# Input projections of a two-layer trunk: dense tiles or steps between the products of the heads

## What is computed

```python
def trunk_layer(x, cond, layer, lp, rope, ctx):
    mod = cond @ lp['w_mod'] + lp['b_mod']
    sh1, sc1, g1, sh2, sc2, g2 = jnp.split(mod[:, None, :], 6, axis=-1)
    hmix = rmsnorm(x, lp['norm1_g']) * (1 + sc1) + sh1
    mix, new_ctx = token_mixers(hmix, layer, lp, rope, ctx)
    x = x + g1 * mix
    hffn = rmsnorm(x, lp['norm2_g']) * (1 + sc2) + sh2
    gate, up = jnp.split(hffn @ lp['w_ffn_in'], 2, axis=-1)
    x = x + g2 * ((jax.nn.silu(gate) * up) @ lp['w_ffn_out'])
    return x, new_ctx

def token_mixers(h, layer, lp, rope, ctx):
    (q_a, k_a, v_a, beta_a, alpha_a, z_a, q_b, k_b, v_b, u_c, gate_logits) = split_columns(h @ lp['w_in'])
    ...
    o_a, s_fin = gated_deltanet(q_a, k_a, v_a, beta_a, alpha_a, z_a, ...)
    o_b, kv = differential_attention(q_b, k_b, v_b, ...)
    o_c = hyena(u_c, ...)
    g_a, g_b, g_c = jnp.split(jax.nn.sigmoid(gate_logits), 3, axis=-1)
    merged = g_a * (o_a @ lp['w_br_a']) + g_b * (o_b @ lp['w_br_b']) + g_c * (o_c @ lp['w_br_c'])
    out = merged @ lp['w_out']
```

## Time and profile before

| what | value |
|---|---|
| median of 3 runs | 4095.87 us (4094.25 to 4096.15) |
| span of the profiled execution | 4092.7 us (3.2 us below the median) |
| PE busy | 3457.7 us, 84% |
| PE's weight loads | 3089.2 us, 75% |
| DVE busy | 1412.5 us, 35% |
| POOL busy | 1435.3 us, 35% |
| ACT busy | 841.8 us, 21% |

### The profile page before, as it was taken

The page is one execution under the profiler, slowest core; times in us unless marked ns, Lnnn a source line. Parts: engine busy times, 40 slices in busy tenths (PEclk is TensorE's granted clock), DMA queues, the critical chain, the costliest instruction groups (busy, mean ns, idle before and its releaser), DMA issues.

```text
span 4092.7 us, 61740 instructions
## 1 busy us (share of the span) xinstructions
PE 3457.7 (84%) x21792; PEld 3089.2 (75%) x21792; DVE 1412.5 (35%) x2231; ACT 841.8 (21%) x1657; POOL 1435.3 (35%) x1088
## 2 busy tenths in 40 slices
PE   6978887777889987999987788887687899799997
PEld 5967767535659987999977676784374799799996
DVE  2066663255531222111122666614553412211112
ACT  3133332232111112000022333313312111210001
POOL 0444442002205543444424444320131255254443
PEclk8988898877799998999988999987787999899998
DMA  4201111111102211222211111111111122121221
GB/s 159 75 29 42 41 41 62 55 41 50 58 27 72 77 66 48 72 72 70 75 64 51 43 41 41 41 62 54 41 55 49 37 77 72 41 77 67 71 73 67
DMA packets 62782, 240.94 MB, mean 59 GB/s; under 512 B 6960, under 2 KB 6960, under 8 KB 61488
## 3 DMA queue, kind: packets, MB, share of 16 engines
q1 hardware_dynamic: 60336, 224.77, 15.9%
q10 hardware_dynamic: 1728, 12.36, 0.8%
q0 software_dynamic: 576, 2.10, 0.1%
HBM read 234.48 MB, written 4.72 MB: 58 GB/s over the span
## 4 chain that ended last, share of the span: by engine, by line
PE 69%; DVE 16%; issue 6%; DVEq 4%; ACT 2%; POOL 1%; ACTq 1%; POOLq 1%; DMA 0%; SPq 0%
PE ps_G L583 26%; PE ps_GPM L583 25%; DVE whi_room L1564 3%; PE ps_GPM L614 3%; DVE outs L1636 2%; PE ps_M L967 2%; DVE outs L1632 2%; PE ps_G L852 1%; DVE small L1756 1%; PE ps_M L909 1%; PE ps_M L891 1%; PE ps_M L664 1%; PE ps_M L995 1%; DVE big L1787 1%; DVEq L1453 1%
## 5 line engine op out<-in xcount | busy, mean ns | idle before, releaser
L1973 POOL CAST w_hi<-ring 128x1024 fp32r<-128x1024 f32 x296 | 309.0, 1044 | 1620.8 <-PE ps_G L583 1002.4
L1975 POOL TENSOR_TENSOR w_lo<-ring,w_hi 128x1024 fp32r<-128x1024 f32 x296 | 740.3, 2501 | 51.1 <-issue 9.1
L583 PE MATMUL ps_G<-room_a,w_hi 128*128 128x320 f32 x1984 | 457.9, 320 | 100.1 <-DVEq L1453 65.4
L583 PE MATMUL ps_GPM<-room_a,w_hi 128*128 128x320 f32 x1984 | 437.5, 309 | 0.0
L583 PEld LDWEIGHTS ps_G<-room_a,w_hi 128*128 128x128 f32 x1984 | 348.5, 197 | 103.0 <-issue 103.0
L583 PE MATMUL ps_G<-room_b,w_hi 128*128 128x320 f32 x1408 | 368.4, 314 | 26.4 <-DVEq L1453 26.4
L583 PE MATMUL ps_G<-room_o,w_hi 128*128 128x320 f32 x1280 | 337.2, 313 | 45.6 <-DVEq L1453 45.6
L583 PE MATMUL ps_GPM<-room_b,w_hi 128*128 128x320 f32 x1408 | 361.4, 309 | 0.0
L583 PE MATMUL ps_GPM<-room_o,w_hi 128*128 128x320 f32 x1280 | 332.9, 309 | 0.0
L583 PEld LDWEIGHTS ps_GPM<-room_a,w_hi 128*128 128x128 f32 x1984 | 331.8, 188 | 0.0
L2027 POOL TENSOR_TENSOR outs<-big,con 128x512 f32<-128x512 f32 x168 | 207.7, 1237 | 350.1 <-DVEq L1602 230.9
(11 more groups left out here) (393 smaller groups left out, 6006.8 us busy)
## 6 DMA issues: line engine op xcount, KB each, us to landing
ring<-in_W SPq DMA_DIRECT2D x416, 512.0 KB, 3.2
big<-in_INV ACTq DMA_DIRECT2D x2, 1664.0 KB, 6.6
par<-in_PARAMS ACTq DMA_DIRECT2D x2, 1646.0 KB, 7.8
big<-in_FWD ACTq DMA_DIRECT2D x2, 1632.0 KB, 8.3
x<-in_X SPq DMA_DIRECT2D x1, 2560.0 KB, 8.8
out_Y<-h SPq DMA_DIRECT2D x1, 2560.0 KB, 7.6
con<-in_CONSTS SPq DMA_DIRECT2D x1, 1364.0 KB, 11.6
sc<-in_HYCS ACTq DMA_DIRECT2D x2, 578.5 KB, 3.7
```

The source lines that it names most:

```text
L583: m = pe.matmul(ap, w[wi][:, k, n0:n0 + P], acts[ai][k][:, a:b], start=(k == 0 and i == 0), stop=(k == chunks - 1 and i == 2))
L1973: nc.gpsimd.tensor_copy(hi, raw)
L1975: nc.gpsimd.tensor_tensor(wlo[:, slot * UNIT:(slot + 1) * UNIT], raw, hi.bitcast(F32), ALU.subtract)
```

## The change

The units are dealt out anew, and with them the places of the products. h's parts get rooms for a whole layer (`h_hi`, `h_lo`), made once at each norm, tile by tile: DVE scales a tile, ACT shifts and rounds it, DVE takes the rest two tiles later; PE's first tile waits chunk by chunk. `round_tiles` and `low_tiles` are gone: A, B, C and mix read the same parts. Each branch's o gets rooms too, and `merged` gets its parts per pair of tiles during the last third of mix; out's first tile waits chunk by chunk. The first third of mix writes `merged` where it was added to zeros before.

Stage A has 7 dense tiles (q, k, v of head 0 and 1 and z of head 0). The other tiles of A, all of B and the values (four tiles by channel, transposed later per head) are 21 tiles that `projection_steps` divides into steps of three matmuls. Delta heads carry 64 steps each, attention heads 0 and 1 32 each and head 2 16. They use one pair of PSUM banks (`G0`, `G1`), which ACT empties by halves (`first_half`, `second_half`). Both sets of heads are written out instead of looped over. The last delta head makes no convolutions, norms and reciprocals; there DVE rotates for attention head 0, before the reciprocal of the output norm. Scores keep two pairs of banks.

Modulation units leave the delta heads (8 each) and stand in norm 1 (8), attention heads 0 to 3 (4, 4, 8, 8), norm 2 (4) and the last step of each f1 group (4 each, between its tiles). `f2`'s first tile waits for its activations chunk by chunk. GpSimd splits two units before a head's levels, one after level 3, one after the last level, then makes the next head's growth factors. The state is stored per head from ACT's queue (before, once by POOL), the rope table is loaded from ACT's queue in the last delta head. In the Hyena stage the eight products of its gate (`gv`) come before the filter's arguments on DVE, and two tables are loaded earlier.

```diff
-    return [("A", 4, "wwww"), ("delta", H, "m" * 8), ("B", 2, "wwww"), ("V", 1, "wwww"), ("attn", H, "mmmm"),
-            ("C", 3, "wwww"), ("mix", 3, "w" * 12), ("out", 2, "wwww"),
-            ("f1_0", 4, "wwww"), ("f2_0", 2, "wwww"), ("f1_1", 4, "wwww"), ("f2_1", 2, "wwww"),
-            ("f1_2", 3, "wwww"), ("f2_2", 2, "wwww")]
+    return [("n1", 1, "m" * 8), ("A0", 1, "w" * 7), ("D0", 1, "wwww"), ("D1", 1, "wwww"), ("D2", 1, "wwww"),
+            ("D3", 1, "wwww"), ("T0", 1, "wmmwmm"), ("T1", 1, "wmmwmm"), ("T2", 1, "w" + "m" * 8), ("T3", 1, "m" * 8),
+            ("C", 3, "wwww"), ("mix0", 1, "w" * 12), ("mix1", 1, "w" * 12), ("mix2", 1, "w" * 12), ("out", 2, "wwww"),
+            ("n2", 1, "mmmm"), ("f1_0", 3, "wwww"), ("fx_0", 1, "wwmmwwmm"), ("f2_0", 2, "wwww"),
+            ("f1_1", 3, "wwww"), ("fx_1", 1, "wwmmwwmm"), ("f2_1", 2, "wwww"),
+            ("f1_2", 2, "wwww"), ("fx_2", 1, "wwmmwwmm"), ("f2_2", 2, "wwww")]
...
-SCORE_BANKS = [("M0", "M1"), ("M2", "M3"), ("G0", "G1")]
-
-ROTATIONS = [("rot_q", "G0"), ("rot_k", "G1")]
+SCORE_BANKS = [("M0", "M1"), ("M2", "M3")]
...
+            def projection_steps(phase, units, fills, first_fill, layer):
+
+
+                def run(a, b):
+                    for s in range(a, b):
+                        u, half, k = s // 16, (s // 8) % 2, s % 8
+                        w = parts(phase, units[u], layer)
+                        if half == 0:
+                            to, lo_, hi_ = over_banks[0][:, 0:HALF], 0, HALF
+                        else:
+                            to, lo_, hi_ = over_banks[0][:, HALF:NT], HALF, NT
+                        if k == 0:
+                            _, fl = fill(fills, "ab"[half], layer, first_fill + u)
+                        for i, (wi, ai) in enumerate(PAIRS):
+                            m = pe.matmul(to, w[wi][:, k, :], h_parts[ai][k][:, lo_:hi_], start=(k == 0 and i == 0),
+                                          stop=(k == KC - 1 and i == 2))
+                            if half == 1 and k == 0 and i == 0:
+                                m.then_inc(fl, 1)
+                        if k == KC - 1 and half == 0:
+                            m.then_inc(filled["G0"], 1)
+                        if k == KC - 1 and half == 1:
+                            m.then_inc(unit_used, 1)
...
+                    project(0, 8)
                     pe.wait_ge(qk_ready.sem, qk_ready.at(Q, 1))
...
+                    project(8, 20)
...
+                        if lev == 1:
+                            project(22, 24)
+                        else:
+                            project(22 + lev, 23 + lev)
...
+                    project(29, 31)
...
+                        base = 31 + 5 * step
...
                         for d in range(2):
...
+                        project(base + 2, base + 4)
...
-                        if step < 2:
-                            mod_units("delta", (4 + 2 * step, 5 + 2 * step), L, hd)
-                    pe.wait_ge(rows_delta.sem, rows_delta.at(Q, 2))
-                    fill("delta", "cols1", L, hd)
-                    turn_rows(mod_rows)
-
+                        project(base + 4, base + 5)
+
+                    project(51, 64)
+                    if hd == H - 1:
+                        swapped(lambda name: fill("rot", name, L), 0)
                     pe.wait_ge(oscaled.sem, oscaled.at(Q, 1))
...
-
-                        mod_units("attn", (qb,), L, hd)
+                        if hd < 2:
+                            project(*((4, 12), (12, 16), (16, 24), (24, 30))[qb])
+                            if qb == 1:
+                                mod_units(T, 0, (0, 1), L)
+                        elif hd == 2:
+                            project(*((3, 6), (6, 9), (9, 12), (12, 16))[qb])
+                        elif qb == 0:
+                            mod_units(T, 0, (1, 2), L)
+                        elif qb == 1:
+                            mod_units(T, 0, (3,), L)
+                        elif qb == 3:
+                            turn_group(T, 0, L, mod_rows_t)
+                            mod_units(T, 1, (0, 1), L)
                         if qb:
                             transposed(qb - 1)
...
-                    swapped(f, hd + 1)
+                    if hd < 2:
+                        project(30, 32)
+                        mod_units(T, 0, (2, 3), L)
+                    elif hd == 2:
+                        mod_units(T, 0, (0, 1, 2, 3), L)
+                    else:
+                        mod_units(T, 1, (2, 3), L)
+                    if hd < H - 1:
+                        swapped(f, hd + 1)
                     transposed(3)
...
-                    pe.wait_ge(rows_attn.sem, rows_attn.at(Q, 1))
-                    fill("attn", "cols0", L, hd)
-                    turn_rows(mod_rows_b)
+                    if hd == 2:
+                        turn_group(T, 0, L, mod_rows_t)
+                        mod_units(T, 1, (0, 1, 2, 3), L)
...
-                pe.wait_ge(h_split.sem, h_split.at(L, 4))
-                pe.sem_inc(passed, 1)
-                with pe.Fori(0, 3) as b:
+                for b in range(3):
                     for half in range(2):
-                        products("mix", f"g{half}_", 6 * half, L, b, h_b)
+                        for t in range(4):
+                            w = parts(f"mix{b}", 6 * half + t, L)
+                            tile_product("mix", f"g{half}_{t}", t, L, b, w, 0, h_parts).then_inc(unit_used, 1)
...
+                products("out", "t", 0, L, 0, m_parts, before=merged_tile)
+                products("out", "t", 0, L, 1, m_parts)
                 sum_squares("norm2", L, hv, KC, sq_ready)
-
-                pe.wait_ge(hf_split.sem, hf_split.at(L, 1))
+                mod_units("n2", 0, range(4), L)
...
+                    for t in range(4):
+                        w = parts(f"fx_{g}", FX_UNITS[t], L)
+                        tile_product(f"fx_{g}", f"t{t}", t, L, 0, w, 0, h_parts).then_inc(unit_used, 1)
+                        if t % 2:
+                            mod_units(f"fx_{g}", 0, (t - 1, t), L)
+                    products(f"f2_{g}", "t", 0, L, 0, act_parts, n, before=act_tile)
...
-            def shift(layer, k0, mod_at):
+            def shift_and_round(layer, k0, mod_at):
 
                 for k in range(KC):
                     act.wait_ge(hnorm.sem, hnorm.at(layer, k0 + k + 1))
-                    nc.scalar.activation(hv[:, k, 0:NS], hv[:, k, 0:NS], ACT.Identity,
+                    nc.scalar.activation(fresh[:, k, 0:NS], fresh[:, k, 0:NS], ACT.Identity,
                                          bias=modv[:, mod_at + k, 0:1])
-                    nc.scalar.activation(hv[:, k, NS:NT], hv[:, k, NS:NT], ACT.Identity,
+                    nc.scalar.activation(fresh[:, k, NS:NT], fresh[:, k, NS:NT], ACT.Identity,
                                          bias=modv[:, mod_at + k, 1:2])
-                act.drain()
+                    act.drain()
+                    nc.scalar.activation(h_parts[0][k], fresh[:, k, :], ACT.Copy).then_inc(hi_ready.sem, 1)
...
                 def scale(i, layer, value):
 
+
+                    def low(k):
+                        dve.wait_ge(hi_ready.sem, hi_ready.at(layer, i * KC + k + 1))
+                        tt(h_parts[1][k], fresh[:, k, :], h_parts[0][k].bitcast(F32), ALU.subtract)
+                        dve.drain().then_inc(lo_ready.sem, 1)
+
                     inverse_rms(i, value)
                     for k in range(KC):
                         for q, (a, b) in enumerate(((0, NS), (NS, NT))):
-                            stt(hv[:, k, a:b], xv[:, k, a:b], gainv[:, i, k, q:q + 1], rstd[:, a:b], ALU.mult, ALU.mult)
+                            stt(fresh[:, k, a:b], xv[:, k, a:b], gainv[:, i, k, q:q + 1], rstd[:, a:b], ALU.mult, ALU.mult)
                         dve.drain().then_inc(hnorm.sem, 1)
+                        if k >= 2:
+                            low(k - 2)
...
                         if step == 3:
...
+                    if last:
+                        dve.wait_ge(rope_in.sem, rope_in.at(L, 16))
+                        rotate(lambda name: drained("rot", name, L), 0)
                     dve.wait_ge(orms.sem, orms.at(Q, 1))
                     nc.vector.reciprocal(orn, orn)
...
+                for j in range(4):
+                    for a, z, at in ((0, NS, 3), (NS, NT, 5)):
+                        tt(ov[:, 8 + j, a:z], PA[:, 4 + j, a + at:z + at], PA[:, 8 + j, a + at:z + at], ALU.mult)
+                    dve.drain().then_inc(gv_ready.sem, 1)
...
+                        tt(o_parts[b][1][k], ov[:, 4 * b + k, :], o_parts[b][0][k].bitcast(F32), ALU.subtract)
...
+                    split(f"D{hd}", (0, 1), L)
                     level(0)
                     level(1)
...
                     for lev in range(2, NLEV):
                         level(lev)
...
+                        if lev == 3:
```

(13 more changed lines are left out.)

1086 lines of the change are left out of this document (593 added, 493 removed).

## The result

The changed kernel takes 3711.72 us (median of four runs, 3708.15 to 3713.21) where the kernel before takes 4095.55 beside it: a ratio of 0.9065, with a 95% interval of 0.9052 to 0.9078. The forecast was 3686 (3600 to 3798). It came within 26 us, but that is luck in good part: over both layers the delta heads gained 51 us more than forecast and attention lost 51 us more, and these two cancel. What is left of the miss lies mostly in norm 1. The profiled execution of after has a span of 3711.1 us, 381.6 less than before.

The account below looks back on a forecast made before the run. PE was taken to bound the kernel, busy 84% of 4092.7 us and idle 635. Terms summed to -205 us a layer, -410 for two; plus 3.2 us for the runs' median, 3686 us (3600 to 3798).

Parts of the forecast that it names:

- The dense tiles that leave: Stages A and B: A goes from 16 tiles to 7, -64.4 us a layer; B goes altogether, -58.2.
- the prologue: Before the first delta head: reciprocals and transposes stay, about 17 of 31.1 us, so -14 a layer.
- hyena's and mix's gaps: Hyena's tail no longer waits for h parts, -9.7 us; mix to out falls from 11.32 to about 2.3, -9.
- +4 for the order in hyena: Hyena: eight products before the filter arguments lie on DVE's chain, +4 us a layer, between 0 and +4.
- +3 a head for the splits: Delta heads: four GpSimd weight splits a head slow DVE's taps, +3 us a head, between 0 and 8.
- A0's end: Sign that the forecast is right: in layer 0 this end comes near 150 us.
- My 105 us: Length of delta heads 0 to 2: 106 + 14.1 - 14.6 - 4 + 3, so -1 a head.
- +6 for its tail: Last delta head: rotation before the output norm's reciprocal leaves waits uncovered, +6 us, between -3 and +12.
- my 214: Attention stage: 214 us for 219, -5 a layer, with 50 us of added PE work.
- my lower bound: Low end of the forecast, -43 us a layer, 3600 us; attention's part, -9, holds its gain of clock.
- head 3 with units alone shrinks to about 48: Attention: its last head, carrying modulation units but no steps, shrinks to about 48 us.
- nearly cancel: Norm 1: modulation units fill PE's wait, beta/alpha follow at full clock; ends -8 and +6 us, taken as -1.

Follow-up runs that it names:

- thinned: Against the changed kernel, each projection step in the delta heads makes one of its three products (hi x hi): 3716.51 us.
- dense kernel: Against the changed kernel, all 64 steps of a delta head run in one piece behind its scan, two GpSimd splits and ScalarE's evacuations moving too: 3878.79 us.

## Why the prediction was right or wrong

**Right, with their reason.** The dense tiles that leave, the prologue (17.3 us, as written), the gap before B, the values, hyena's and mix's gaps (no gap over 3.8 us is left at mix and out), +4 for the order in hyena (3.8 and 1.9 come back when it changes), and +3 a head for the splits (2.6 for their subtractions). That PE's idle time takes the steps in held for delta heads 0 to 2, at a clock of 1.00; in attention it did not hold. Of the signs that I named, A0's end (155.5 for 150) and the heads (100.6 us, 91% busy) came; the last head (91.5 for 104) and attention (238.9 for 214) did not. One reading was loose: in stage C GpSimd is busy 38.0 of 86.2 us, which is not most of the time.

**Delta heads 0 to 2: the clock's term was too small.** My 105 us are 96.8 of busy time (86.7 + 14.1 - 4) and 7.8 of waits (19.4 - 14.6 + 3). Head 1 has 91.4 and 9.1. So the cover, net of the splits, came out nearly as counted: 10.3 us for 11.6. What is off is the clock: 86.7 - 14.5 + 28.6 would be 100.8 us of busy time, so it gave back 9.4 us where I took 4. The rows allowed more: 86.7 us at the head's mean clock of 0.90 are 78 at 1.00, which gives 8.7 (an estimate). Nor do the two terms stand alone, as the thinned and the dense kernel show: with fewer products in the waits, or all steps in one place, the clock is 0.92 and 0.89, and the head is no shorter.

**Head 3: a wrong step.** I gave it +6 for its tail and took 2 us of PE's work off it for the next head's norms that it no longer makes. The tail did cost 5.4 us more (8.19 to 13.61). But in before, head 3 ran VectorE's taps and reciprocals for a next head as well; with them gone VectorE is busy 44.5 us instead of 64.4, the levels take 44.2 for 48.8, and the scan 18.2 for 23.3. I had taken that work for free because it wasn't PE's. Its rows fit this account, but it is argued: no run puts that work back.

**Attention: the cover failed.** I added 50 us of PE's work to 147.6, and my 214 leaves 16 of the 71 us of waits. Measured are 62.8 us of waits, so 8.5 us were covered where I counted 55. The stage lost no more because PE is busy 176.1 us, not 198, at a clock that rose from 0.75 to 0.87; I had that in my lower bound alone. By heads I had 51.5, 51.5, 58, 48 and 5 for the end; measured are 53.1, 57.5, 62.5, 64.2 and 1.7. The step that failed by most (16.2 of the 24.9 us) is "head 3 with units alone shrinks to about 48": it counted PE's work and left out that all units share one bank, which VectorE frees behind its maxima and combinations. The bank is 4 to 6 us of it by experiment. The rest of heads 2 and 3 goes when the number and the places of units change together. Head 1's 6 us are steps in front of its scores and a collision with GpSimd, as far as the traces show.

**Norm 1: "nearly cancel" failed.** The units did run at full clock, 14.1 us. Three things unpriced stand behind them. The first tile takes 15.0 us for 7.2: it goes chunk by chunk behind VectorE, which splits hold up twice. The beta/alpha products, which I put at 8.6 us at full clock, take 13.45 at 0.65. And the tile behind them takes 9.2 us. The kernels with both halves per chunk and with beta/alpha in pieces win 3.9 and 6.3 us at just these places in layer 0, together about the miss of 10.4.

## What to carry to other kernels

When work is moved into waits, price the wait that the moved-out work leaves as well, and ask for each engine, not for the bounding one alone, what leaves its chain. Where pieces stand counts as much as their sum: 64 steps of 0.45 us spread over a 100 us chain cost it nothing net of the clock they kept up, in a row they cost 22 us, and a head gave back 11 us when the eight units in its tail became four between its blocks. A run that thins such work shows its price only if the clock stays; look at it first. Before trusting a sum over PE's work, look for a buffer that all the moved work shares, and at who frees it.
